# Two weight rings of a decoder-block kernel moved by 16 and 64 bytes inside SBUF

## What is computed

```python
def squared_relu_mlp(hn, w_up, w_down):
    return jnp.square(jax.nn.relu(hn @ w_up)) @ w_down

def first_block(x, ...):
    h = x
    for i in range(DEPTH):                       # DEPTH = 2
        hn = rmsnorm(h, mix_norm_g[i])
        mix = gated_deltanet(hn, dn_w_in[j], ...) if i % 2 == 0 else moba_layer(hn, mb_w_in[j], mb_w_out[j])
        h = h + mix
        h = h + squared_relu_mlp(rmsnorm(h, mlp_norm_g[i]), mlp_w_up[i], mlp_w_down[i])
    return rmsnorm(h, final_norm_g)

def second_block(x, mem, ...):
    h = _rms_norm(x, norm_mix_pre[l])
    a_q, ..., s_c = jnp.split(h @ w_in[l], cuts, axis=-1)
    ...
    gates = jax.nn.sigmoid(h @ w_gate[l] + b_gate[l])
    mixed = jnp.sum(gates * proj, axis=2) @ w_out[l]
    x = x + _rms_norm(mixed, norm_mix_post[l])
    ...
    yff = (jax.nn.silu(u_g) * u_v) @ w_down[l]
    return x + _rms_norm(yff, norm_ffn_post[l])
```

## Time and profile before

| | |
|---|---|
| device time, median of 3 runs | 1251.89 us (1251.63 to 1254.33) |
| span of the profiled execution | 1249.1 us, first to last instruction |
| its own device time | not listed; the runs lie 2.5 to 5.2 us above the span |
| TensorE busy (matmuls) | 1220.7 us, 98% of the span |
| TensorE weight loads | 1106.9 us, 89%, beside the matmuls |
| VectorE, ScalarE, GpSimd busy | 70%, 56%, 5% |
| DMA | 210.80 MB, mean 169 GB/s |

### The profile page before, as it was taken

One profiled execution on the slowest core, in us unless ns is written; L12 is line 12 of the kernel. 1 busy time (PEld: TensorE's weight loads), 2 busy tenths in 40 slices (PEclk: granted clock), 3 DMA queues, 4 the chain that ended last, 5 costly groups with the idle time before them and its releaser, 6 DMA issues.

```text
span 1249.1 us, 21521 instructions
## 1 busy us (share of the span) xinstructions
PE 1220.7 (98%) x8583; PEld 1106.9 (89%) x8583; DVE 871.6 (70%) x1252; ACT 700.5 (56%) x1016; POOL 56.3 (5%) x102
## 2 busy tenths in 40 slices
PE   8999989999999999999999999999999999999997
PEld 7999988888888998888888999999999977888886
DVE  5888567666666656666656589998656577778876
ACT  4984555555455554554554564656454456666663
POOL 5010020000000001000000000000000010000000
PEclk9999999999999999999999999999999999999999
DMA  7671134666554654565555565354546534555561
GB/s 223 197 203 68 38 122 150 222 214 202 186 184 151 203 165 141 166 211 180 184 185 167 172 210 184 118 162 145 179 150 203 186 107 147 174 194 190 201 201 68
DMA packets 160340, 210.80 MB, mean 169 GB/s; under 512 B 5542, under 2 KB 143220, under 8 KB 160261
## 3 DMA queue, kind: packets, MB, share of 16 engines
q1 hardware_dynamic: 157315, 202.77, 50.6%
q0 software_dynamic: 1904, 6.85, 1.4%
q10 hardware_dynamic: 1042, 0.07, 0.1%
HBM read 208.62 MB, written 1.05 MB: 168 GB/s over the span
## 4 chain that ended last, share of the span: by engine, by line
PE 79%; DVE 10%; ACT 4%; issue 2%; DMA 2%; SPq 1%; POOL 1%; DVEq 0%; POOLq 0%; ACTq 0%
PE bank L369 16%; PE bank L373 16%; PE bank L372 16%; PE bank L454 15%; PE bank L450 8%; DVE wlo L305 3%; ACT whi L297 2%; PE bank L1425 2%; DMA raw<-in_dn_w_in 1%; DVE common L2582 1%; PE bank L2003 1%; PE bank L1445 1%; ACT common L753 1%; SPq L3388 1%; PE bank L2095 1%
## 5 line engine op out<-in xcount | busy, mean ns | idle before, releaser
L305 DVE TENSOR_TENSOR wlo<-raw,whi 128x2048 fp32r<-128x2048 f32 x190 | 434.9, 2291 | 203.6 <-ACT whi L297 203.3
L297 ACT ACTIVATE whi<-raw 128x2048 fp32r<-128x2048 f32 x190 | 363.3, 1913 | 145.4 <-PE bank L369 43.5
L369 PE MATMUL bank<-xparts,whi 128*128 128x256 f32 x912 | 262.5, 288 | 0.4 <-DVE common L2764 0.4
L373 PE MATMUL bank<-xparts,wlo 128*128 128x256 f32 x912 | 258.7, 284 | 0.0
L372 PE MATMUL bank<-xparts,whi 128*128 128x256 f32 x912 | 258.6, 284 | 0.0
L454 PE MATMUL bank<-xparts,whi 128*128 128x512 f32 x832 | 208.0, 392 | 0.0
L369 PEld LDWEIGHTS bank<-xparts,whi 128*128 128x128 f32 x912 | 175.5, 192 | 2.8 <-issue 2.1
L372 PEld LDWEIGHTS bank<-xparts,whi 128*128 128x128 f32 x912 | 175.6, 192 | 0.6 <-issue 0.5
L373 PEld LDWEIGHTS bank<-xparts,wlo 128*128 128x128 f32 x912 | 175.5, 192 | 0.0
L454 PEld LDWEIGHTS bank<-xparts,whi 128*128 128x128 f32 x832 | 149.8, 189 | 26.9
L369 PE MATMUL bank<-whi,hhi 128*128 128x512 f32 x392 | 153.1, 391 | 3.8 <-DVE hlo L1061 2.3
(11 more groups left out here) (391 smaller groups left out, 1706.2 us busy)
## 6 DMA issues: line engine op xcount, KB each, us to landing
raw<-in_mlp_w_up SPq DMA_DIRECT2D x32, 1024.0 KB, 5.5
raw<-in_mlp_w_down SPq DMA_DIRECT2D x32, 1024.0 KB, 5.1
raw<-in_w_in SPq DMA_DIRECT2D x22, 1024.0 KB, 5.3
raw<-in_w_up SPq DMA_DIRECT2D x22, 1024.0 KB, 5.2
raw<-in_w_gate SPq DMA_DIRECT2D x16, 1024.0 KB, 5.5
raw<-in_dn_w_in SPq DMA_DIRECT2D x15, 1024.0 KB, 5.8
raw<-in_mb_w_in SPq DMA_DIRECT2D x12, 1024.0 KB, 5.2
raw<-in_w_down SPq DMA_DIRECT2D x11, 1024.0 KB, 4.9
```

The costliest lines, as they stand in the source:

```text
L297: nc.scalar.activation(whi[:, s, :], raw[:, r, :], ACT.Copy).then_inc(hi_ready, 1)
L305: nc.vector.tensor_tensor(wlo[:, s, :], raw[:, V % RAW, :], f32(whi[:, s, :]), ALU.subtract).then_inc(lo_ready, 1)
L369: ins = pe.matmul(o, shi, mhi, start=first, stop=False, skip_group_check=True)
L373: return pe.matmul(o, slo, mhi, start=False, stop=last, skip_group_check=True)
```

## The change

Each ring is allocated 32 elements (128 bytes) longer, and the part of it that is used begins 4 elements (16 bytes) into `whi` and 16 elements (64 bytes) into `wlo`. `xparts` also becomes 128 bytes longer and still begins at its start; `hhi` and `hlo` keep their size. So `wlo` lies 128 bytes further on before its own shift, `xparts` 256 bytes, all behind it 384 bytes: multiples of 128 that leave every other tensor as far past a multiple of 128 as before. No instruction is added, removed or put in another order, and no shape or type changes.

```diff
-        whi = sb("whi", [P, RING, UNIT], F32R)
-        wlo = sb("wlo", [P, RING, UNIT], F32R)
-        xparts = sb("xparts", [P, 2, KT, T], F32R)
+        PAD, W_AT, X_AT, H_AT = 32, (4, 16), 0, (0, 0)
+        whi, wlo = (sb(n_, [P, RING * UNIT + 32], F32R)[:, at_:at_ + RING * UNIT]
+                    .rearrange("p (s n) -> p s n", s=RING) for n_, at_ in zip(("whi", "wlo"), W_AT))
+        xparts = sb("xparts", [P, 2 * KT * T + PAD], F32R)[:, X_AT:X_AT + 2 * KT * T]\
+            .rearrange("p (x k t) -> p x k t", x=2, k=KT)
         xhi, xlo = xparts[:, 0], xparts[:, 1]
-        hhi = sb("hhi", [P, 2, 2, T], F32R)
-        hlo = sb("hlo", [P, 2, 2, T], F32R)
+        hhi, hlo = (sb(n_, [P, 4 * T + 0], F32R)[:, at_:at_ + 4 * T]
+                    .rearrange("p (a b t) -> p a b t", a=2, b=2) for n_, at_ in zip(("hhi", "hlo"), H_AT))
```

## The result

The changed kernel takes 1256.54 us (median of 9 runs, 1253.72 to 1258.51), the kernel before, run beside it, 1252.82 us (9 runs, 1251.24 to 1254.73). The ratio is 1.0032, with a 95% interval of 1.0022 to 1.0041. The forecast of 1246 us had the wrong sign. Of its rivals "rows pay more than features gain" came nearest, in part by luck, as is shown further down.

A forecast was written before the change was run, and what follows sets the result against it. TensorE's matmul stream was taken to bound the kernel, each matmul perhaps held up by the next weight load. Terms 7.7 + 1.3 + 0.7 - 4.0 gave 5.7 us less, so 1246 us, range 1232 to 1261 us.

The forecast's parts named there:

- rows pay more than features gain: Rival: 512-column ring matmuls lose more than 256-column ones gain; 3.3 us longer, 1255 us, up to 1264 us; chance 0.26.
- The premise on places: Whole blocks of 128 bytes between operands were taken as neutral; only places past a multiple of 128 were to count.
- Items 4 and 5: Rows and 512-column tokens: 3.3 ns more each, 4.0 us more; L454: no change, ends 2.7 us either way.
- Items 1 to 3: 256-column matmuls against the rings get shorter: features 7.7 us less, L450 1.3 us less, tokens 0.7 us less.
- Items 6 and 7: `bhi`/`blo` with the rings: no change, ends 1.3 us more and 1.0 less; ring writes by ScalarE and VectorE: priced at nothing.
- The last step: From TensorE to whole time: only first units of each stage wait and do not shorten, so nearly all 5.7 us arrives.
- point of decision: The rows rival decides once the 2,056 long matmuls lose over 9.7 us, 4.7 ns each.
- Nothing happens: Rival: read ports are independent or only whole 128-byte blocks count, so time stays at 1252 us; chance 0.20.
- The hold-up mostly goes: Rival: pairs with the high ring loaded lose half their excess (13.3 and 16.7 ns), 19 us less, 1233 us; chance 0.12.

The follow-up runs named there:

- streams alone: Kernels of matmul streams only, operands at chosen byte places, other engines silent; the aligned pair took 120.0 ns (256 columns) and 226.7 ns (512).
- the one with the shortest span: Against the kernel before: rings, `hhi`, `hlo` 64 bytes past `xparts` modulo 512, `bhi`/`blo` 64 bytes before the rings modulo 256; ratio 0.9934.
- the kernel with the common 16 bytes: The change's pads kept, but both rings, `hhi` and `hlo` all moved by 16 bytes; ratio 1.0020 against the kernel before.
- 64-byte layout: Instead of the change, both rings, `hhi` and `hlo` begin 64 bytes past `xparts` modulo 512; 1243.24 us, 0.9922 of the kernel before.

## Why the prediction was wrong

**The premise on places failed.** "Multiples of 128 that leave every other tensor as far past a multiple of 128 as before" was true and beside the point: pads of 256 bytes change nothing, pads of 128 move rows by 2.9 ns, so what counts is the distance of the two operands modulo 256. By that the "64 bytes" of `wlo` beside `xparts` were 192, and rows met 112 and 192. The "32 bytes" of `bhi` and `blo` were 224 where they move and 32 where they are loaded, and their "16 and -32" after the change were, where they move, 112 and 32. So the prices were taken from pairs at 0, 32 and 224 for distances of 16, 112 and 192. This alone does not make the miss: the shifts without the pads, where the distances are those that it named, brought no gain either (1.0004).

**Items 4 and 5, rows and L454, were put too low, and together they turn the sign.** For rows 3.3 ns were taken from 0 to 6.6; 5.3 came, 6.2 us over the 1,164 dense pairs with `hhi` and `hlo` where 4.0 us stood for all. The reason given, that no one standing holds where the products of a triple meet different distances, is refuted: the triple alone settles at 231.1 or 232.2 ns. For L454 "no change" was taken and its worse end, 2.7 us, came. Its 230.0 ns in the kernel before were read as the middle of a range that the shift would not leave; it was the pitch that alternation gives at distance 0 (streams alone: 230.3), and 233.7 in streams at the new places. From the 5.7 us less of the sum to the 2.0 us more of the trace, these two make 4.9 us, features and L450 2.4 us, the other ring matmuls 0.3.

**Items 1 to 3 had the right sign.** Features gained 2.0 ns instead of 2.8 (5.7 us, not 7.7), L450 0.9 us instead of 1.3, tokens the 0.7 us expected. **Items 6 and 7** held in their result: +0.2 us for `bhi` and `blo`, and 2289 ns for the split.

**The last step, "nearly all of the 5.7 us should arrive", failed as well.** It looked at loads and splits at the start of a stage. The transposes behind features wait for VectorE and ScalarE; the waits of those two stretches grew by 2.6 us in the changed kernel, some 2 us of it behind features, and by 5.8 in the one with the shortest span.

**The rivals.** "Rows pay more than features gain" had its terms nearly right: 233 ns for rows and L454, 2.2 ns gained by features, 1255 us. Its point of decision, 4.7 ns lost by each long matmul, was about reached (5.3 and 3.3 ns) with a smaller gain on the other side. That its 3.3 us come so near to the measured 3.7 is in part luck: the pitches give 2.0, and the waits and the clock, which it did not count, the rest. Against it stood that wide half units lose only half, which was a reading of L454's alternation as a shift. "Nothing happens" fell: nearly every pitch moved, and the Trainium skill's two independent read ports ("TensorE: Matmul & The Clock Gate", section "Step-by-step: what each phase is for") do not go with 113.3 to 120.0 ns for one matmul by the place of its operands alone. Nor did any stream reach the 109.2 and 215.8 ns of its section "Wait — 56ns, not 53.3ns?"; the least were 113.3 and 226.7. "The hold-up mostly goes" needed half of 13.3 ns; the distance 64 gives half (6.7 ns), but features did not get that distance.

**What is open.** Ring pitches give +2.0 us, and waits and one stretch at the lower clock the rest of the 4.6 us between two single profiled executions. That the clock falls there in other executions of the changed kernel was not shown. It is not the bulk of the 0.3%: executions with a mean granted clock of 0.998 took 1253.72 to 1257.66 us in the changed kernel and 1250.36 to 1252.08 us in the kernel before (run beside the experiments). The rule of the distance modulo 256 is shown for places at multiples of 64 bytes; the changed kernel, with `whi` at 16, is explained by streams at its very places and not by the rule. Of the rows in the kernel with the common 16 bytes (232.7 ns) no stream was run. Why a distance has the pitch it has was not found.

## What to carry to other kernels

Where TensorE runs dense, the place of an operand in SBUF is a tuning parameter: measure the pitch of the very pair (columns, order of products) as a stream by itself, and set loaded against moving modulo 256 bytes for each use, since one tensor meets several partners and the best distance for one width can be the worst for another. Padding by whole blocks of 128 bytes is not neutral, by 256 it was here; check it against what the pads do alone. A layout chosen by the streams brought 0.8%, half of what they promised. A gain on TensorE counts in full only where nothing behind it waits for another engine.

## What the runs showed of the hardware beyond that

- The same matmul, same operands, same neighbours, has more than one steady pitch: 113.33 or 117.78 ns at the distance 64, chosen by how the stretch begins and kept to its end. The longest stretch of features, 335 matmuls, stands at 113.4 ns in the 64-byte layout and at 117.8 with all of it 64 bytes further on.
- Steps under 16 bytes count too: the loaded operand 4 bytes further on gives 118.4 ns and 8 bytes 115.5 for 256 columns, 232.4 and 230.6 for 512.
- The distance is not all: at 16/16 and 48/48 bytes, distance 0, 512 columns take 231.1 ns instead of 226.7 and 256 columns 116.7 and 118.3 instead of 120.0, while 32/32, 64/64 and 128/128 give 226.7 and 120.0. At 80/16, distance 64, 512 columns take 228.9 ns, not 233.3.
